# Trunk step on one Trainium2 core: small work of the attention stage goes from VectorE to GpSimd, and rows, score pieces and loads are issued in another order

## The reference

```python
p = softmax(q @ k.T * scale (+ bias))          # A: neighbourhood attention with a 2-D bias, 4 heads
p = softmax(q1 @ k1.T) - lam * softmax(q2 @ k2.T)   # B: differential attention, lam from four small vectors
p = softmax(concat(q @ k.T * scale + mask, sink))   # D: banded attention with a learned sink logit
o = p @ v                                      # latent tokens see latents and 512 cached keys, context tokens see themselves
```

## Time and profile before

| | |
|---|---|
| median of 3 runs (lowest, highest) | 3809.15 us (3808.78, 3819.94) |
| the profiled execution: time, span, mean granted TensorE clock | 3812.29 us, 3811.0 us, 0.974 |
| busy over the span: PE, PEld, DVE, ACT, POOL | 3604.6, 2705.1, 2051.8, 802.9, 1150.2 us |
| attention of layer 0 (404 to 850 us): PE, DVE, ACT, POOL busy | 400.9, 260.3, 207.8, 356.9 us |
| attention of layer 1 (2262 to 2708 us): PE, DVE, ACT, POOL busy | 399.9, 260.8, 208.8, 357.0 us |

### The profile page before, as it was taken

One profiled execution on the slowest core, in us unless ns is written; L12 is line 12 of the kernel. 1 busy time (PEld: TensorE's weight loads), 2 busy tenths in 40 slices (PEclk: granted clock), 3 DMA queues, 4 the chain that ended last, 5 costly groups with the idle time before them and its releaser, 6 DMA issues. The chain is left out here.

```text
span 3811.0 us, 47904 instructions
## 1 busy us (share of the span) xinstructions
PE 3604.6 (95%) x19082; PEld 2705.1 (71%) x19082; DVE 2051.8 (54%) x3224; ACT 802.9 (21%) x1284; POOL 1150.2 (30%) x728
## 2 busy tenths in 40 slices
PE   6999899889999999999989998988899999999998
PEld 4788433446888888888868963344488888888886
DVE  5223555654666666666573156556536555545455
ACT  3111344451200000000032124544311000000003
POOL 0010589672211111111131128987331111111113
PEclk8999899899999999999999999999999999999998
DMA  6754253335112212212215544234421011011111
GB/s 228 246 178 134 64 138 96 113 110 187 39 50 78 74 44 78 78 39 78 68 55 168 162 128 106 83 106 110 152 87 45 34 45 36 32 45 45 34 34 56
DMA packets 267718, 350.45 MB, mean 92 GB/s; under 512 B 66878, under 2 KB 194064, under 8 KB 267368
## 3 DMA queue, kind: packets, MB, share of 16 engines
q1 hardware_dynamic: 236560, 332.75, 27.9%
q10 hardware_dynamic: 30936, 14.64, 1.8%
HBM read 279.99 MB, written 72.16 MB: 92 GB/s over the span
## 5 line engine op out<-in xcount | busy, mean ns | idle before, releaser
L2371 PE MATMUL bank<-h_hi,w_hi 128*128 128x512 f32 (+1 forms) x2496 | 905.6, 363 | 30.6 <-issue 26.0
L2372 PE MATMUL bank<-h_lo,w_hi 128*128 128x512 f32 (+1 forms) x2496 | 889.7, 356 | 0.0
L2373 PE MATMUL bank<-h_hi,w_lo 128*128 128x512 f32 (+1 forms) x2496 | 889.6, 356 | 0.0
L2189 DVE SCALAR_TENSOR_TENSOR xT<-bank,mods,xT 128x512 f32<-128x512 f32 (+1 forms) x816 | 533.8, 660 | 268.1 <-PE bank L2373 256.4
L2371 PE MATMUL bank<-m_hi,w_hi 128*128 128x512 f32 (+1 forms) x1536 | 555.4, 362 | 18.0 <-DVE xT L2189 17.7
L2371 PEld LDWEIGHTS bank<-h_hi,w_hi 128*128 128x128 f32 x2496 | 476.0, 191 | 112.5 <-issue 43.9
L2373 PE MATMUL bank<-m_hi,w_lo 128*128 128x512 f32 (+1 forms) x1536 | 550.0, 358 | 0.0
L2372 PE MATMUL bank<-m_lo,w_hi 128*128 128x512 f32 (+1 forms) x1536 | 549.3, 358 | 0.0
L2372 PEld LDWEIGHTS bank<-h_lo,w_hi 128*128 128x128 f32 x2496 | 476.3, 191 | 72.1 <-issue 5.3
L2373 PEld LDWEIGHTS bank<-h_hi,w_lo 128*128 128x128 f32 x2496 | 475.6, 191 | 67.1
L920 POOL TENSOR_SCALAR w_hi<-stage 128x2048 fp32r<-128x2048 f32 x90 | 173.5, 1928 | 1050.1 <-issue 526.9
(11 more groups left out here) (210 smaller groups left out, 4092.6 us busy)
## 6 DMA issues: line engine op xcount, KB each, us to landing
stage<-in_w_mlp SPq DMA_DIRECT2D x64, 1024.0 KB, 5.3
nx_w<-in_w_ada SPq DMA_DIRECT2D x16, 1536.0 KB, 9.3
stage<-in_w_in SPq DMA_DIRECT2D x18, 1024.0 KB, 6.3
ada_h<-in_w_ada SPq DMA_DIRECT2D x16, 1024.0 KB, 8.1
rope_t<-in_k_rope SPq DMA_DIRECT2D x28, 512.0 KB, 4.4
rden<-s_rden ACTq DMA_DIRECT2D x28, 320.0 KB, 4.6
ada_w<-in_w_ada SPq DMA_DIRECT2D x4, 2048.0 KB
stage<-in_w_out SPq DMA_DIRECT2D x8, 1024.0 KB, 6.5
```

The source lines that it names most:

```text
L2189: dve.scalar_tensor_tensor(out=x, in0=bank[:, bk, :n], scalar=mods[l][:, gate + k, cd:cd + 1], in1=x, op0=ALU.mult, op1=ALU.add).then_inc( ...
L2371: x = pe.matmul(out, a_hi, b_hi, start=first, stop=False)
L2372: pe.matmul(out, a_hi, b_lo, start=False, stop=False)
L2373: return x, pe.matmul(out, a_lo, b_hi, start=False, stop=last)
```

## The change

GpSimd makes lambda and the sinks at the start of the attention stage, `sinks(1)` before the steps of job 18, and the nine lower parts of A's and D's output one slot after ACT made the high parts. `PIECE_LEAD` goes from 4 to 3, so pieces from slot 0 on come one slot later (where no other limit holds them). The maxima row comes after the slot's scores, always in bank 7; ACT copies it after the slot's first exponential and sends it after the last. The denominators' way is one slot later in its second half for all but the seventh group. The table na_q of A's second pair of heads (8 DMAs) is loaded while the first A group runs, not at the start of the first D group, where it stood ahead of the next heads. DVE waits for the new semaphores where it uses lambda, the sinks and the rings of the tail.

```diff
-ROW_LEAD, PIECE_LEAD, HEAD_LEAD = 2, 4, 4
+ROW_LEAD, PIECE_LEAD, HEAD_LEAD = 2, 3, 4
...
-ROW_BANK = [third(s + 1) + 1 for s in ROW_AT]
+ROW_BANK = [7] * NJ
...
-RECIP_AT = {FIRST_SLOT[(v + 1) * NCH] + 4: v for v in range(NV - 1)}
+RECIP_AT = {FIRST_SLOT[(v + 1) * NCH] + 4 + (v < NV - 2): v for v in range(NV - 1)}
...
 # sync: the loop over v
-                if kind == "D" and h2 == 0:
-                    sp.wait_ge(s1_max, l * 2 * PIECES + 2 * PIECE0[v * NCH])
-                    settle(sp)
-                    load_bias(sp, l, 1, 0)
                 if v and v + 1 < NV:
                     load_head(sp, l, v + 1)
...
                         store_out(JOBS[(v - 1) * NCH][0], JOBS[(v - 1) * NCH][1], cc)
+                if kind == "A" and h2 == 0:
+                    sp.wait_ge(s1_max, l * 2 * PIECES + 2 * PIECE0[(v + 1) * NCH])
+                    settle(sp)
+                    load_bias(sp, l, 1, 0)
                 denominators_out(v * NCH + 1)
...
 # gpsimd, after its memsets
+            pool.wait_ge(lam_e, l + 1)
+            pool.tensor_tensor(lam_s[:, 4:5], lam_s[:, 3:4], lam_s[:, 2:3], ALU.subtract).then_inc(lam_d, 1)
+            pool.tensor_scalar(lam_s[:, 6:7], lam_i, -1.0, 1.0, ALU.mult, ALU.add).then_inc(lam_d, 1)
+            pool.wait_ge(lam_d, l * 5 + 4)
+            pool.tensor_tensor(lam_s[:, 5:6], lam_s[:, 4:5], lam_i, ALU.subtract)
+            pool.tensor_tensor(sub_g[:, 1:2], sub_g[:, 0:1], lam_s[:, 6:7], ALU.mult).then_inc(lam_d, 1)
+            sinks(0)
...
             for s in range(STEPS):
+                if SLOT_OF[s] - 1 in PAIR_AT and s == STEP0[SLOTS[SLOT_OF[s]][0]] + SLOTS[SLOT_OF[s]][1][0]:
+                    lower_pair(*PAIR_AT[SLOT_OF[s] - 1])
+                if s == STEP0[D_JOBS[2] + 1]:
+                    pool.wait_ge(m_col, l * NJ + D_JOBS[2] + 1)
+                    sinks(1)
...
+            for s in sorted(PAIR_AT):
+                if s >= NS - 1:
+                    lower_pair(*PAIR_AT[s])
             scale(NV - 1)
...
 # scalar
-                if s in ROW_AT:
-                    max_row(ROW_AT.index(s))
-                    send_row(ROW_AT.index(s))
                 if s < NS:
                     for i in SLOTS[s][1]:
                         exponentials(SLOTS[s][0], i)
+                        if s in ROW_AT and i == SLOTS[s][1][0]:
+                            max_row(ROW_AT.index(s))
+                if s in ROW_AT:
+                    send_row(ROW_AT.index(s))
...
 # vector: the loop over slots
-                if s == 6:
-                    lambda_now()
-                    sinks(0)
                 if s in RECIP_AT:
                     invert(RECIP_AT[s])
-                if s in PAIR_AT:
-                    lower_pair(*PAIR_AT[s])
...
 # tensor: the loop over slots
+                    for i in steps:
+                        scores(j, i)
                     if s in ROW_AT:
                         max_row(ROW_AT.index(s))
-                    for i in steps:
-                        scores(j, i)
```

More of the change, by code:

```diff
@@ L308, in bank_users @@
             order += [("piece", g, x, (piece_banks(g)[x],)) for g in SLOT_PIECES[s][:2] for x in range(2)]
-            order += [("row", j, 0, (ROW_BANK[j],)) for j in range(NJ) if ROW_AT[j] == s]
             for i in SLOTS[s][1]:
@@ L312, in bank_users @@
                 order.append(("step", si, 0, (step_bank(si), step_bank(si) + 1)))
+            order += [("row", j, 0, (ROW_BANK[j],)) for j in range(NJ) if ROW_AT[j] == s]
         order += [("den", g, 0, (DEN_BANK[g],)) for g in range(NSUM) if SUM_AT[g] == s]
@@ L491 @@
 DEN_IN_AT = {FIRST_SLOT[(v + 1) * NCH] + 3: v for v in range(NV - 1)}
-RECIP_AT = {FIRST_SLOT[(v + 1) * NCH] + 4: v for v in range(NV - 1)}
-RDEN_OUT_AT = {FIRST_SLOT[(v + 1) * NCH] + 5: v for v in range(NV - 1)}
-RDEN_IN_AT = {FIRST_SLOT[(v + 1) * NCH] + 6: v for v in range(NV - 1)}
-SCALE_AT = {FIRST_SLOT[(v + 1) * NCH] + 8: v for v in range(NV - 1)}
-PAIR_AT = {FIRST_SLOT[(v + 1) * NCH] + 9 + c: (v, c) for v in PAIRS if v < NV - 1 for c in range(NCH)}
+RECIP_AT = {FIRST_SLOT[(v + 1) * NCH] + 4 + (v < NV - 2): v for v in range(NV - 1)}
+RDEN_OUT_AT = {FIRST_SLOT[(v + 1) * NCH] + 5 + (v < NV - 2): v for v in range(NV - 1)}
+RDEN_IN_AT = {FIRST_SLOT[(v + 1) * NCH] + 6 + (v < NV - 2): v for v in range(NV - 1)}
+SCALE_AT = {FIRST_SLOT[(v + 1) * NCH] + 8 + (v < NV - 2): v for v in range(NV - 1)}
+PAIR_AT = {FIRST_SLOT[(v + 1) * NCH] + 9 + (v < NV - 2) + c: (v, c) for v in PAIRS if v < NV - 1 for c in range(NCH)}
 A_TAB = 7 * 16
@@ L1418, in _, with sinks, lower_pair @@
             pool.wait_ge(a_init, l * 6 + 6)
+            def sinks(h2):
+                for x in range(2):
+                    put_in = pool.tensor_scalar(mps[:, :, x, :, 0], zero8.rearrange("p (i t) -> p i t", i=2),
+                                                sink_c[:, 2 * h2 + x:2 * h2 + x + 1], None, ALU.add)
+                put_in.then_inc(sink_cols, 1)
+            pool.wait_ge(lam_e, l + 1)
[5 more added lines that the diff above has]
+            sinks(0)
+            def lower_pair(v, c):
+                c0, n = CHUNKS[c]
+                idx = pair_index(v, c)
+                ring = idx % NAO_RING
+                pool.wait_ge(ao_h, l * NAO + idx + 1)
+                pool.tensor_tensor(ao_lo[ring][:, :n], o_ad[:, c0:c0 + n], ao_hi[ring][:, :n].bitcast(F32), ALU.subtract).then_inc(ao_l, 1)
             def scale(v):
@@ L2046, in maxima @@
                 dve.wait_ge(s1_max, l * 2 * PIECES + 2 * PIECE0[j + 1])
+                if kind == "D":
+                    dve.wait_ge(sink_cols, l * 2 + JOBS[j][1] + 1)
                 if j >= 2:
@@ L2080, in invert @@
                     dve.reciprocal(den_1, den_c).then_inc(den_inv, 1)
+                    dve.wait_ge(lam_d, l * 5 + 5)
                     dve.wait_ge(den_inv, l * 2 + JOBS[v * NCH][1] + 1)
@@ L2101, in more_sum @@
                 dve.tensor_tensor(den_sb[j % 2][:, :n], den_sb[j % 2][:, :n], bank[:, DEN_BANK[g], :n], ALU.add).then_inc(den_more, 1)
-            def sinks(h2):
-                for x in range(2):
-                    dve.tensor_scalar(mps[:, :, x, :, 0], zero8.rearrange("p (i t) -> p i t", i=2), sink_c[:, 2 * h2 + x:2 * h2 + x + 1],
-                                      None, ALU.add)
-            def lambda_now():
-                dve.wait_ge(lam_e, l + 1)
-                dve.wait_ge(a_tab, (l + 1) * A_TAB)
-                dve.tensor_tensor(lam_s[:, 4:5], lam_s[:, 3:4], lam_s[:, 2:3], ALU.subtract).then_inc(lam_d, 1)
-                dve.tensor_scalar(lam_s[:, 6:7], lam_i, -1.0, 1.0, ALU.mult, ALU.add).then_inc(lam_d, 1)
-                dve.wait_ge(lam_d, l * 5 + 4)
-                dve.tensor_tensor(lam_s[:, 5:6], lam_s[:, 4:5], lam_i, ALU.subtract)
-                dve.tensor_tensor(sub_g[:, 1:2], sub_g[:, 0:1], lam_s[:, 6:7], ALU.mult).then_inc(lam_d, 1)
-                dve.wait_ge(lam_d, l * 5 + 5)
             def piece_at(s, x):
@@ L2123, in piece_at @@
                         maxima(PIECE_JOB[g][0])
-                    if g + 1 == PIECE0[D_JOBS[2] + 1]:
-                        dve.wait_ge(m_col, l * NJ + D_JOBS[2] + 1)
-                        sinks(1)
-            for s in range(NS + 1):
+            for s in range(NS):
                 if s < NS:
@@ L2155, in _ @@
                 dve.tensor_scalar(g_neg[:, m], bank[:, m, 256:512], -1.0, None, ALU.mult).then_inc(f_g, 1)
+            dve.wait_ge(ao_l, l * NAO + (len(PAIRS) - 1) * NCH)
+            dve.wait_ge(lam_d, l * 5 + 5)
             for x in range(2 * NCH):
```

2 lines of the change are left out of this document (1 added, 1 removed).

## The result

The changed kernel takes 3788.82 us (median of 6 runs, 3784.07 to 3796.3) where the kernel before took 3813.28 beside it: ratio 0.994, 95% interval 0.993 to 0.995. That is 24 us less where 54 were forecast, and outside the range, 2 us above its end. (The forecast was counted from the 3809.15 us of three earlier runs; from the 3813.28 of these six it would be 3759.) The profiled execution took 3787.89 us, span 3786.6, mean granted clock 0.978.

What follows compares the result with a forecast made beforehand. PE, busy 95% of the span, was taken as the bound, so only its waits could be won: 36.0 gained less 9.0 lost is 27 us a layer, 54 in both, giving 3755 us; range 3736 to 3787.

Steps and rivals of the forecast that it cites:

- (a): Added POOL work, lower parts and tiny operations, delays sums PE needs: 2.0 us a layer lost, 0 to 10.
- (b): Maxima rows sent behind both exponentials come late, at A and D heads and job 23: 5.5 us a layer lost.
- (4): First D part, slots 66 to 69: group 6's keys no longer wait behind eight bias DMAs; 10.5 us a layer gained.
- (5): Lower parts moved off DVE, slots 73, 84 and 85: PE's waits for DVE go, 4.2 us a layer gained.
- (1): Lambda and sinks moved off DVE, slot 7: 13.4 us becomes 4.7, 8.7 us a layer gained.
- (2): First pieces of head groups 2 and 3, slots 17 and 30: a slot later, load waits go; 8.6 us a layer gained.
- (3): Slot 57: `invert` one slot later removes DVE's wait for `den_c` and PE's for DVE; 4.0 us a layer gained.
- My rival on GpSimd: GpSimd becomes the bound, half of (1), (2) and (5) comes back as waits for `acc`: 3775 us, chance 0.12.
- rows late at the crowded jobs: Rows beside bulk loads take 8.75 us, jobs 13, 16, 19, 22 lose 5 each, keys no sooner: 3787 us, chance 0.17.

Runs made afterwards that it cites:

- the combination: Changed kernel with GpSimd's scales moved and two adds fewer, group 7's heads ahead of stores, pieces and rows a slot sooner from job 13: 3761.5 us, 0.9846.

## Why the prediction was wrong

The waits that were to go went, but the losses (a) and (b) were put too small, the gains (4) and (5) too large, and the wait for group 7's keys was not in the sum. Of the 27.0 us a layer 12.4 came. Against the forecast (a) cost 7.6 more and (b) 4.2, (4) gave 3.8 less and (5) 2.4; the first three gains and the slots not named gave 3.4 more.

*Gains.* (1), (2) and (3), 21.3 us a layer, came in full, 21.8. But (2) was argued wrongly: I wrote that the pieces one slot later simply lose their wait. Alone the lead brought 10 us where (2) and (3) were to bring 25; it needs the row in bank 7, which I had booked as a cost only. And (3) counted slot 57 alone, where with the lead of 3 the later `invert` also spares a wait in slot 18.

(4) was to give 10.5 a layer and gave 6.7 (5.4 in layer 1). The keys came as said; what took it back is the row of job 16, 3.54 us in slot 67. "The rest is the row of job 16 and `den_c`, which may stay" priced it as it was before, not as it would be sent behind both exponentials, beside the bias load.

(5) was to give 4.2 and shows as 1.8 in its slots, but undoing it cost some 9 us in both layers, and 6 in the combination, neither of them clear of the intervals. By these it is near the forecast.

*Losses.* (a) is the step that failed most: "I take 2.0 more (0 if the slot's shift of `scale` spares it, 10 if all of the lower parts' time shows)". It cost 9.6 a layer in slots 35 to 41 and 63, at the end of my bound of 10, and the shift does not spare it but makes it: with the shift undone 1.0 a layer is left. Nor is it the moved work: with the lead, the shift and the later row on the kernel before, and all small work still on DVE, the same slots take 45.3 us for the 45.4 of the change (35.7 before). The working had the numbers for a stretch without slack, 53 to 56 us of GpSimd's work against 53.5 of PE's in a B head group; what it did not ask is where in it the burst of `scale` stands. In the old slot the sum of slot 36 is due next and PE waits 1.55 us; a slot later group 1's stands right ahead of the adds for the sum of slot 39, and group 3's in the last slot of job 13, whose sum is due in slot 63; their waits are 3.25 and 3.71 us, with the clock at 0.50 of 2.4 GHz behind both. Placing and cutting GpSimd's work otherwise gave 15 us back in the two layers. My rival on GpSimd had the place, and with "half of (1), (2) and (5)", 10 a layer on top of the 2.0, a price near the 7.6 measured; but its cause, POOL's work beside a PE that no longer waits, holds for some 1.0 of the 9.6, and its 3775 let the rest of the sum stand.

(b), 5.5 a layer, was right for B and too small for A and D: 9.7 in slots 56, 78, 79, 88 to 91 and 94, some of it the keys', and 3.5 more inside (4). The rival "rows late at the crowded jobs" named the price of a row beside bulk loads, and the rows measured 7.4 and 8.4 us from issue to use. But it took 16 us a layer more for them than the forecast, where some 8 at most are the rows'. That it came near in time (3787 for 3789) is luck: GpSimd's 7.6 made up the difference.

Missing altogether: the stores of group 4's output. I counted what SyncE's loads are moved past, but not that the pairs a slot later, and the lower parts in GpSimd's queue, hold the stores, and that group 7's keys stand behind these. The wait for them cost 1.74 us in slot 78 (3.54 in layer 1), and 8.01 once the pieces were a slot sooner.

The forecast's own range, 3736 to 3772, does not follow from its terms. "12 us less in both layers" is 3779 if it is meant for each layer and 3767 if for both, not 3772, and "all of 36.0 kept" is 3737. The loss (a) was left out of it, though its bound was 10.

The combination shows that the three corrections together are worth what was missing: 30 us were missing in the two stages, and they give 34.5. It does not prove that they are the whole of it. They also take away two adds a layer that the forecast had counted, and waits of the kernel before, and DVE waits of 1.87 and 1.79 us stand in the end that the forecast did not have. The shares are 15 us for GpSimd, 3.5 to 12 for the keys alone and nothing to 16 for the rows, by what else is corrected; the intervals of the ratios are 5 us wide to either side.

## What to carry to other kernels

When a change takes waits out of a stage, put the next engine's work per unit beside the shortened time of that unit, and then ask where its bursts stand: an engine without slack cannot hide 6 us of other work ahead of a result that is due, and one slot can decide over which result that is. When an operation is moved or delayed, follow what is queued behind its consumers too (here a lower part, a store, and a load behind the store). One edit that shifts several operations can win with one and lose with another: undo them one by one. A part that costs time alone can be the one that lets another pay, so measure pairs, not only parts. And where a change touches a fifth of the time, compare that stretch too, since the rest varied by up to 17 us here, where the change is worth 24.
